# Expert weights: one matrix per slab with four rows per partition, 256-column groups

## The reference

```python
def expert_choice_ffn(h, w_router, w_gate_e, w_up_e, w_down_e):
    cap = CAPACITY_FACTOR * N // N_EXPERTS            # 32
    aff = jax.nn.softmax((h @ w_router).astype(jnp.float32), axis=-1)
    top_aff, top_idx = lax.top_k(aff.transpose(0, 2, 1), cap)
    xg = h[bidx, top_idx]
    a = jnp.einsum("becd,edf->becf", xg, w_gate_e)
    u = jnp.einsum("becd,edf->becf", xg, w_up_e)
    out = jnp.einsum("becf,efd->becd", jax.nn.silu(a) * u, w_down_e) * top_aff[..., None]
    return jnp.zeros_like(h).at[bidx, top_idx].add(out)
```

## Time and profile before

| | us |
|---|---|
| median of 3 runs | 2263.96 (2261.31 to 2264.39) |
| the profiled execution | 2266.87 |
| its span | 2265.0 |
| PE busy (matmul) | 1969.0, 87% |
| DMA, mean rate | 254 GB/s |
| L1178, matmuls, busy | 382.5 |
| L1212, matmuls, busy | 117.7 and 66.1 |

### The profile page before, as it was taken

The page is one execution under the profiler, slowest core; times in us unless marked ns, Lnnn a source line. Parts: engine busy times, 40 slices in busy tenths (PEclk is TensorE's granted clock), DMA queues, the critical chain, the costliest instruction groups (busy, mean ns, idle before and its releaser), DMA issues.

```text
span 2265.0 us, 30108 instructions
## 1 busy us (share of the span) xinstructions
PE 1969.0 (87%) x12745; PEld 1076.5 (48%) x12745; DVE 782.7 (35%) x1742; ACT 433.6 (19%) x1095; POOL 26.8 (1%) x52
## 2 busy tenths in 40 slices
PE   6999999998988998889999876667776799999997
PEld 4444644455443333335868531233432347564755
DVE  2587865243112212231364412100110235333533
ACT  2122711022110111012351111000000222222222
POOL 3000000000000000000000000000000000000000
PEclk9999999999999999999999987988998999999999
DMA  8544236315999999992327479999999833233320
GB/s 292 216 164 148 106 112 223 149 74 223 358 423 423 422 419 423 422 403 101 114 110 288 187 329 423 424 415 416 415 415 419 344 111 112 102 122 111 112 84 19
DMA packets 133827, 575.93 MB, mean 254 GB/s; under 512 B 7448, under 2 KB 16128, under 8 KB 92736
## 3 DMA queue, kind: packets, MB, share of 16 engines
q1 hardware_dynamic: 129312, 556.82, 62.1%
q0 software_dynamic: 3872, 17.00, 2.2%
q10 hardware_dynamic: 512, 0.19, 0.0%
HBM read 572.93 MB, written 1.05 MB: 253 GB/s over the span
## 4 chain that ended last, share of the span: by engine, by line
PE 54%; DMA 20%; issue 8%; PEld 7%; DVE 6%; PEldq 3%; ACT 2%; SPq 0%; POOL 0%; DVEq 0%; ACTq 0%; POOLq 0%
DMA ring<-w_up_e 15%; PE ps L834 10%; PE ps L1178 5%; PE ps L1268 5%; PE ps L1004 4%; PE ps L850 4%; PE ps L1276 3%; PEld ps L1212 3%; DMA ring<-w_down_e 3%; PE ps L1410 2%; PE ps L823 2%; PEldq L763 2%; PEld ps L1055 1%; DMA ring<-w_xkv 1%; PE ps L1247 1%
## 5 line engine op out<-in xcount | busy, mean ns | idle before, releaser
L1178 PE MATMUL ps<-ring,reg_bc 128*32 128x512 f32 x2960 | 382.5, 653 | 132.1 <-DMA ring<-w_up_e 124.2
L1178 PEld LDWEIGHTS ps<-ring,reg_bc 128*32 128x32 f32 x2960 | 93.3, 115 | 397.2 <-DMA ring<-w_up_e 206.6
L834 PE MATMUL ps<-reg_a,ring 128*128 128x512 f32 (+1 forms) x768 | 255.0, 488 | 3.3 <-issue 3.3
L834 PEld LDWEIGHTS ps<-reg_a,ring 128*128 128x128 f32 x768 | 143.2, 190 | 102.7 <-issue 91.7
L2386 DVE TENSOR_TENSOR xall<-xall,ps 128x512 f32<-128x512 f32 x48 | 32.8, 686 | 448.2 <-PE ps L1144 448.2
L2429 DVE TENSOR_TENSOR reg_a<-ps,reg_e 32x256 f32<-32x256 f32 x192 | 80.7, 420 | 195.3 <-PE ps L1212 192.9
L1268 PE MATMUL ps<-ring,reg_a 128*128 128x512 f32 (+2 forms) x448 | 142.7, 474 | 2.6 <-issue 2.3
L1761 ACT ACTIVATE reg_bc<-ps 128x512 f32<-128x512 f32 x48 | 28.7, 597 | 568.6 <-PE ps L1178 568.6
L1212 PE MATMUL ps<-ring,reg_bc 128*32 128x256 f32 x2048 | 117.7, 380 | 15.9 <-issue 14.5
L823 PE MATMUL ps<-ring,reg_a 128*128 128x512 f32 (+1 forms) x288 | 112.8, 546 | 1.9 <-issue 1.5
L1268 PEld LDWEIGHTS ps<-ring,reg_a 128*128 128x128 f32 x448 | 74.0, 190 | 65.1 <-issue 63.6
(11 more groups left out here) (375 smaller groups left out, 2302.7 us busy)
## 6 DMA issues: line engine op xcount, KB each, us to landing
ring<-w_down_e SPq DMA_DIRECT2D x64, 2048.0 KB, 14.8
ring<-w_gate_e SPq DMA_DIRECT2D x123, 1024.0 KB, 10.7
ring<-w_up_e SPq DMA_DIRECT2D x123, 1024.0 KB, 13.7
ring<-w_in SPq DMA_DIRECT2D x34, 2048.0 KB, 9.6
ring<-w_ada SPq DMA_DIRECT2D x24, 2048.0 KB, 11.0
ring<-w_out SPq DMA_DIRECT2D x8, 2048.0 KB, 9.0
ring<-w_xkv SPq DMA_DIRECT2D x8, 1024.0 KB, 15.3
ring<-w_br_global SPq DMA_DIRECT2D x4, 1024.0 KB, 8.9
```

The source lines that it names most:

```text
L834: mm = pe.matmul(ps[j][:, 0:n], w[:, k, j * P:(j + 1) * P], HT[:, k, 0:n], start=(k == 0), stop=(k == KC - 1))
L1178: mm = pe.matmul(ps[s][32 * j:32 * j + 32, :], XGT[l][:, e // 4, s, 2 * q + k, e % 4 * CAP:(e % 4 + 1) * CAP], w[j // 2][:, k, (j % 2) * C ...
```

## The change

A gate/up slab now holds 512 rows of one matrix, four neighbouring rows (16 KB) per partition, in one DMA: slabs 0 and 1 are gate, slabs 2 and 3 up. A down slab becomes two DMAs, each of 256 rows with two rows (8 KB) per partition. The early loads bring the same slabs in two DMAs of 8 KB per partition. Column group j takes 256 neighbouring columns j x 256 of the matrix, so that a slab and set has 4 rows x 4 groups of 256 columns; gate fills columns 0 to 255 of the bank and up 256 to 511. The order of the model dimension changes with it: `paired` picks every fourth column of a block of 512, `PAIRED` has 12 rows turned by four transposes, and `WR` is loaded in that order. The wait for the second half of the gathered rows moves from the third slab to the second. The transposes of `GU` read every second column, and the hidden rows (`EG`, `RG`, `HE`) are contiguous, with down picking its 32 columns out of them.

```diff
     def paired(k):
-        return slice(k // 2 * 2 * P + k % 2, (k // 2 + 1) * 2 * P, 2)
+        return slice(k // 4 * 4 * P + k % 4, (k // 4 + 1) * 4 * P, 4)
...
+    def gate_or_up(l, e, part):
+        rows4 = a[("w_gate_e", "w_up_e")[part // 2]][l, e, 4 * P * (part % 2):4 * P * (part % 2 + 1), :]
+        return rows4.rearrange("(p k) n -> p k n", p=P)
...
             if part < 4:
-                return [(c0, 2, D, a[name][l, e, 2 * P * part:2 * P * (part + 1), :].rearrange("(p k) n -> p k n", p=P))
-                        for c0, name in ((0, "w_gate_e"), (2 * D, "w_up_e"))]
+                return [(0, 4, D, gate_or_up(l, e, part))]
             half = a["w_down_e"][l, e, 4 * P * (part - 4):4 * P * (part - 3), :]
-            return [(0, 4, D, half.rearrange("(p k) n -> p k n", p=P))]
+            return [(2 * D * j, 2, D, half[2 * P * j:2 * P * (j + 1), :].rearrange("(p k) n -> p k n", p=P)) for j in range(2)]
...
-            for half, name in zip(EARLY_AT[l, q], ("w_gate_e", "w_up_e")):
-                load(half.rearrange("p (k n) -> p k n", k=2),
-                     a[name][l, 1, 2 * P * q:2 * P * (q + 1), :].rearrange("(p k) n -> p k n", p=P), f"early{l}{q}")
+            for n, half in enumerate(EARLY_AT[l, q]):
+                load(half.rearrange("p (k n) -> p k n", k=2), gate_or_up(l, 1, q)[:, 2 * n:2 * n + 2, :], f"early{l}{q}")
...
-            for i in range(2):
-                pe.transpose(ps[0][:, P + 24 * i:P + 24 * (i + 1)], PAIRED[:, i:2 * P:2], ident[0:24, 0:24])
+            for i in range(4):
+                pe.transpose(ps[0][:, P + 12 * i:P + 12 * (i + 1)], PAIRED[:, i:4 * P:4], ident[0:12, 0:12])
...
-                    if q % 2 == 0 and e % 4 == 0:
-                        pe.wait_ge(*at(f"xgt@{l}", (e // 4 + 1) * 2 * ns - 1 + q // 2))
+                    up, half = q // 2, q % 2
+                    if q < 2 and e % 4 == 0:
+                        pe.wait_ge(*at(f"xgt@{l}", (e // 4 + 1) * 2 * ns - 1 + q))
...
-                        for k in range(2):
+                        for k in range(4):
                             for j in range(4):
-                                mm = pe.matmul(ps[s][32 * j:32 * j + 32, :],
-                                               XGT[l][:, e // 4, s, 2 * q + k, e % 4 * CAP:(e % 4 + 1) * CAP],
-                                               w[j // 2][:, k, (j % 2) * COL:(j % 2 + 1) * COL],
-                                               start=(q == 0 and k == 0), stop=(q == 3 and k == 1))
+                                mm = pe.matmul(ps[s][32 * j:32 * j + 32, up * SEQ:(up + 1) * SEQ],
+                                               XGT[l][:, e // 4, s, 4 * half + k, e % 4 * CAP:(e % 4 + 1) * CAP],
+                                               w[k // 2][:, k % 2, j * SEQ:(j + 1) * SEQ],
+                                               start=(half == 0 and k == 0), stop=(half == 1 and k == 3))
...
-                        mm = pe.transpose(ps[2 + s][:, c * P:(c + 1) * P], GU[l][:, s, c:COL:4], ident[:, :])
+                        mm = pe.transpose(ps[2 + s][:, c * P:(c + 1) * P], GU[l][:, s, c // 2 * SEQ + c % 2:(c // 2 + 1) * SEQ:2], ident[:, :])
...
-                                               HE[l][:, s, k, q * CAP:(q + 1) * CAP],
+                                               HE[l][:, s, k % 2 * P + (2 * q + k // 2) * CAP:k % 2 * P + (2 * q + k // 2 + 1) * CAP],
```

More of the change, by code:

```diff
@@ L256, in build @@
         GU.append(reg_bc[:, gu:gu + ns * COL].rearrange("p (s n) -> p s n", s=ns))
-        EG.append(reg_bc[:, eg:eg + ns * SEQ].rearrange("p (s c n) -> p s c n", s=ns, c=4))
-        RG.append(reg_bc[:, rg:rg + ns * SEQ].rearrange("p (s c n) -> p s c n", s=ns, c=4))
+        EG.append(reg_bc[:, eg:eg + ns * SEQ].rearrange("p (s n) -> p s n", s=ns))
+        RG.append(reg_bc[:, rg:rg + ns * SEQ].rearrange("p (s n) -> p s n", s=ns))
         hidden = reg_e[:, 1024:1280] if he is None else reg_bc[:, he:he + ns * SEQ]
-        HE.append(hidden.rearrange("p (s c n) -> p s c n", s=ns, c=4))
+        HE.append(hidden.rearrange("p (s n) -> p s n", s=ns))
         OE.append(reg_a[:, 0:2048 * ns].rearrange("p (b s d) -> p b s d", b=2, s=ns))
-    PAIRED = reg_e[0:24, 0:2 * P]
+    PAIRED = reg_e[0:12, 0:4 * P]
     YT = reg_e[:, 4096:5120].rearrange("p (b n) -> p b n", b=2)
@@ L671, in _ @@
                      a[f"diff_lambda_{v}_2"][l:l + 1, :].broadcast_to([P, 32]), "ld_const")
-            load(WR[:, l].rearrange("p (q i) e -> p q i e", i=2), a["w_router"][l].rearrange("(q p i) e -> p q i e", p=P, i=2), "ld_const")
+            load(WR[:, l].rearrange("p (q i) e -> p q i e", i=4), a["w_router"][l].rearrange("(q p i) e -> p q i e", p=P, i=4), "ld_const")
         for t in range(2):
@@ L1164, in experts @@
                         pe.wait_ge(sem(f"early{l}{q}"), 32)
-                        gate_up = EARLY_AT[l, q]
+                        pairs2 = EARLY_AT[l, q]
                     else:
@@ L1168, in experts @@
                         slab_wait(pe, i)
-                        gate_up = slot(i)[:, 0:2 * D], slot(i)[:, 2 * D:4 * D]
-                    w = [half.rearrange("p (k n) -> p k n", k=2) for half in gate_up]
-                    if q % 2 == 0 and e % 4 == 0:
-                        pe.wait_ge(*at(f"xgt@{l}", (e // 4 + 1) * 2 * ns - 1 + q // 2))
+                        pairs2 = slot(i)[:, 0:2 * D], slot(i)[:, 2 * D:4 * D]
+                    w = [two.rearrange("p (k n) -> p k n", k=2) for two in pairs2]
+                    up, half = q // 2, q % 2
+                    if q < 2 and e % 4 == 0:
+                        pe.wait_ge(*at(f"xgt@{l}", (e // 4 + 1) * 2 * ns - 1 + q))
                     for s in range(ns):
@@ L1769, in experts @@
                     act.wait_ge(*at(f"gu_turned@{l}", m + 1))
-                    gate = ps[2 + s][:, :].rearrange("p (c n) -> p c n", c=4)[:, :, 0:2 * CAP]
-                    act.activation(EG[l][:, s], gate, ACT.Sigmoid).then_inc(sem(f"eg@{l}"), 1)
+                    act.activation(EG[l][:, s], ps[2 + s][:, 0:SEQ], ACT.Sigmoid).then_inc(sem(f"eg@{l}"), 1)
                 if e < 12:
@@ L1942, in _ @@
             for n, v in enumerate((a["b_ada"][l, 3 * D:4 * D], a["b_ada"][l, 4 * D:5 * D], a["norm2_g"][l])):
-                load_vec("ld_vec0", PAIRED[12 * l + 4 * n:12 * l + 4 * n + 4, :], v.rearrange("(q c) -> q c", c=2 * P))
+                load_vec("ld_vec0", PAIRED[6 * l + 2 * n:6 * l + 2 * n + 2, :], v.rearrange("(q c) -> q c", c=4 * P))
         act.wait_ge(*at("vec1t", 1))
@@ L2073, in bias_columns @@
             link(dve.tensor_copy(vec0t[:, :], ps[0][:, 0:P]))
-            pairs_in = ps[0][:, P:P + 48].rearrange("p (i l n q) -> p l n q i", i=2, l=DEPTH, n=3)
+            pairs_in = ps[0][:, P:P + 48].rearrange("p (i l n q) -> p l n q i", i=4, l=DEPTH, n=3)
             for l in range(DEPTH):
                 for n, c in enumerate((24, 32, 56)):
-                    ins = dve.tensor_copy(vec0t[:, 64 * l + c:64 * l + c + 8].rearrange("p (q i) -> p q i", i=2),
+                    ins = dve.tensor_copy(vec0t[:, 64 * l + c:64 * l + c + 8].rearrange("p (q i) -> p q i", i=4),
                                           pairs_in[:, l, n])
@@ L2409, in experts @@
                     m = e * ns + s
-                    turned = ps[2 + s][:, :].rearrange("p (c n) -> p c n", c=4)
                     dve.wait_ge(*at(f"eg@{l}", m + 1))
-                    dve.tensor_tensor(RG[l][:, s], EG[l][:, s], turned[:, :, 0:2 * CAP], ALU.mult
+                    dve.tensor_tensor(RG[l][:, s], EG[l][:, s], ps[2 + s][:, 0:SEQ], ALU.mult
                                       ).then_inc(sem(f"rg@{l}"), 1)
@@ L2416, in experts @@
                         dve.wait_ge(*at(f"down@{l}", m - ns + 1))
-                    dve.tensor_tensor(HE[l][:, s], RG[l][:, s], turned[:, :, 2 * CAP:4 * CAP], ALU.mult
+                    dve.tensor_tensor(HE[l][:, s], RG[l][:, s], ps[2 + s][:, SEQ:COL], ALU.mult
                                       ).then_inc(sem(f"hid@{l}"), 1)
```

## The result

The changed kernel takes 2284.43 us (median of four runs, 2283.45 to 2285.57), the kernel before 2264.18 beside it (four runs, 2261.31 to 2265.41). The ratio is 1.0085 with an interval of 1.0073 to 1.0096: slower by about 20 us, and outside the predicted range of 2257.5 to 2271.

The account below looks back on a forecast made before the run. DMA was taken to pace both expert stages, PE close behind. Packets -3.8, instruction blocks +4.0 and PE +0.2 sum to +0.4 us: 2267.3 for the profiled execution, 2264.4 carried to the median; range 2257.5 to 2271.

Parts of the forecast that it names:

- Parts that I cost at nothing: Gather, turnings, hidden rows, waits and DMA counts: taken as free; gather's bounds 0 and 0.8 us in layer 0.
- the load lies under the matmul before it: Gather ahead of each expert stage: weight loads at stride 4 are covered; bounds 0 and 16 x 13 ns per gather.
- mean slack of 1.4 us per expert: Layer 0, 610 to 1010 us: PE waits 18.3 us for up halves, 1.4 for each of 13.3 experts.
- C: Layer 0's experts: PE becomes the bound, from 0.34 us more per slab; with 0.92, about 2301 us; chance 0.05.
- B's end: Both expert stages' DMA stream: 21.7 added instruction blocks at up to 1.09 us each, 2284.0 us; rival's chance 0.15.
- packet term: Expert stages' DMA stream: 16 KB runs save 0.075 us a slab, net 51 slabs, -3.8 us; bounds 0 and -9.2.
- The doubled matmuls: L1178 on PE: 16 matmuls of 256 columns for 8 of 512, +0.02 us a slab, +0.2 us in all.
- the 128 foretold: PE's instruction queue: about 128 blocks of 16 KB after the change, 103 before.
- The fetching: Saturated expert stretches: 21.7 added instruction blocks at 0.186 us each, +4.0 us; bounds +1.5 and +23.7.
- The sum of these terms: Whole kernel: -3.8 for packets, +4.0 for instruction blocks, +0.2 on PE, together +0.4 us.

## Why the prediction was wrong

**The step that failed** stands in "Parts that I cost at nothing": the gather at stride 4 was taken from the row of L1199, 209 ns at stride 4, with 13 ns a load as its upper bound, and only for the four gathers ahead of the stage's first matmul. L1199 is a transpose, and transposes are spared; a matmul's weight load at that step takes 330 ns, 134 more. A row with the same step is not the same operation. And the sentence "the load lies under the matmul before it" did not hold: of the 134 ns more a load, 116 show in a piece (1.85 us over 16 records). The bound was wrong for a second reason: it left out the gather pieces inside the experts, which the timeline shows in each of twelve experts. There the growth is 1.85 us, over the mean slack of 1.4 us per expert that the prediction itself had found.

**A part was not costed at all.** "A part of the modulation vectors" moves to steps of 4 on the moving side; six places at 0.43 us, some 2 us by the end of layer 0's mixer, +3.6 us (1.4 to 5.7) of the whole when this part was put into the kernel before alone. The working went over the turnings and the gather and never over L721.

The Trainium skill ("SBUF — State Buffer", Specifications) says that SBUF is read in lines of 16 bytes and that full bandwidth needs at least two hits in a line. By that rule fp32 at every 2nd column is free and at every 4th is not, and more steps add nothing. The gather's loads agree, 192, 196, 330 and 335 ns at steps of 1, 2, 4 and 8, and so do the modulation products; the transposes don't: 140 ns contiguous, 209, 212 and 193 at 2, 4 and 8. This rule speaks against the change and was not weighed in the prediction.

**The rivals.** C, PE becomes the bound of layer 0, named the right place and the right sign to look for (the waits for slabs almost gone), and had the wrong cause: L1182's busy time did not grow, the gather's did. Its chance of 0.05 was that of its cause. Its threshold was too kind as well, since the mean slack of 1.4 us mixes two kinds of experts. The first two gathering experts have no wait for a slab at all, before or after: from expert 0's turning to expert 2's 53.90 us became 57.75, the full 2 x 1.85 and a little. PE's waits in the kernel before over the next ten experts, from 607.2 to 909.4 us:

```profile
PE ps L1178 <- DMA ring<-w_up_e: 11.6, 14, 1.4
```

That is 1.16 us of slack an expert; the other 6.7 of the 18.3 us stand in the three experts that gather nothing. With 1.85 us on top, 0.69 an expert should be left, and these ten grew by 0.91 (302.23 to 311.33 us together); the 0.2 between stays open. B's end, 2284.0, is the measured time by accident: with three quarters of its instructions alone the kernel stays within 3.6 us of before.

**What held.** The packet term of -3.8: measured alone -4.8 (-7.5 to -2.0), and in layer 1 of the changed kernel the slabs land 4.89 to 4.91 us apart, an expert in 29.53 us (before: 29.65):

```profile
1394.40 2.83 PE L1182 MATMUL ps<-ring,reg_bc 128*32 128x256 f32 x32 [2.96 <-DMA ring<-w_gate_e]
1399.29 3.30 PE L1182 MATMUL ps<-ring,reg_bc 128*32 128x256 f32 x32 [2.06 <-DMA ring<-w_gate_e]
1404.20 1.93 PE L1182 MATMUL ps<-ring,reg_bc 128*32 128x256 f32 x32 [1.62 <-DMA ring<-w_up_e]
1409.09 3.52 PE L1182 MATMUL ps<-ring,reg_bc 128*32 128x256 f32 x32 [2.95 <-DMA ring<-w_up_e]
...
1423.93 1.93 PE L1182 MATMUL ps<-ring,reg_bc 128*32 128x256 f32 x32 [2.20 <-DMA ring<-w_gate_e]
```

The doubled matmuls cost PE next to nothing: 378.9 us for 382.5, and two slabs back to back 7.42 us as forecast, by PE's timeline of the kernel after:

```profile
967.25 7.42 PE L1182 MATMUL ps<-ring,reg_bc 128*32 128x256 f32 x128 [0.29 <-issue]
```

And 127 blocks were fetched for the 128 foretold. The fetching was sized at +4.0, and its sign isn't shown: 4608 of the 6144 added instructions, 3.0 by that price, came to between -0.7 and +3.6 with +1.4 in the middle. The Trainium skill ("Runtime: NRT & Kernel Launch", Instruction fetch mechanics) calls this cost mostly hidden; the middle of these runs lies about halfway between nothing and my price, and their interval holds both. The sum of these terms, +0.4, is what the changed kernel shows once both stepped reads are back at 2 (0.9999, interval 0.999 to 1.0007). The sum held within what can be measured; the list that it was taken over was too short.

Open: why transposes are spared (in the traces each transpose leaves one record and each matmul of the gather two, so the two are not the same work, but no run here shows that this is the reason), whether it is the run length or the number of DMAs that the packet term measures, and how much of the packet gain the added instructions take, which the runs leave as intervals. In layer 0's gathering experts the packet gain can't show, since PE is the bound there.

## What to carry to other kernels

When a layout changes, list every read of every operand whose step changes, and price each from a row of the same operation with the same step; where there is none, leave both ends in the range, since a transpose and a matmul with the same access pattern differ by 120 ns here. Ask of every engine how much slack it has per period beside the bound, and add all growth on it, including small pieces between the main loops: 1.85 us in a period of 30 turned the bound around. A reorder that moves to another engine has to be priced there: moved whole to VectorE it cost 6 us more than on PE, while six writes of the tokens alone were cheap. And a mean slack over a stage hides that the periods with extra work have less of it: 1.16 us here, not 1.4.

## What the runs showed of the hardware

PE's reads of fp32 from SBUF at 4 columns' step run at about 0.6 of the speed at 2 columns' step in matmuls, on both sides: weight load 196 to 330 ns, a moving operand of eight matmuls of 128 columns 0.67 to 1.10 us; at 8 columns 335 ns, no worse. Transposes are not slowed (212 and 193 ns), but have their own step between contiguous (140 ns) and every 2nd column (209). VectorE's fp32 scalar_tensor_tensor of 512 goes from 745 to about 1040 ns (14 in 14.62 us) when read and written in the permuted order, and its tensor_scalar of 1024 from 812 to 1200. A slab of 2 MB lands in 4.90 us in runs of 16 KB (one DMA) and in 4.97 in runs of 8 KB (two DMAs), whichever matrix it is.
